# The first mixer's projections and attention: the context's query projection moved in among x's attention units

## The reference, cut to what matters

```python
aq, bq, ak, av, bk, bv = split_cols(h @ w_in, AB_SPLITS)
aq = apply_rope2d(rms_norm(aq..., a_q_norm), *rope);  ak likewise
y_a = windowed_sink_attention(aq, ak, av, ak_c, av_c, a_sink)
bq = diff_qk(bq, b_q_norm, rope);  bk likewise            # norm per head, rotation
s = einsum(q, k) * HEAD_DIM ** -0.5; p = softmax(s)       # diff_attend
w = p[:, :, 0] - lam * p[:, :, 1];   y_b = w @ v
y_b = rms_norm(y_b, b_sub_norm) * (1 - lam_init)
y = concatenate([y_a, y_b]) @ w_out
# the context: the same without rotation, over its own keys alone
```

## Time and profile before

| what | us |
|---|---|
| median of 3 runs | 2525.12 |
| profiled execution, device time | 2524.71 |
| its span | 2522.8 |
| PE busy in the span | 2451.0 (97%) |
| DVE busy | 1649.8 (65%) |
| ACT busy | 1031.2 (41%) |

### The profile page before, as it was taken

One profiled execution on the slowest core, in us unless ns is written; L12 is line 12 of the kernel. 1 busy time (PEld: TensorE's weight loads), 2 busy tenths in 40 slices (PEclk: granted clock), 3 DMA queues, 4 the chain that ended last, 5 costly groups with the idle time before them and its releaser, 6 DMA issues. The chain is left out here.

```text
span 2522.8 us, 37350 instructions
## 1 busy us (share of the span) xinstructions
PE 2451.0 (97%) x15262; PEld 2147.1 (85%) x15262; DVE 1649.8 (65%) x2728; ACT 1031.2 (41%) x1677; POOL 0.2 (0%) x4
## 2 busy tenths in 40 slices
PE   8999899999999999998899999999999999999999
PEld 8998799899978888886678888888888887879999
DVE  7667544788776677568768666548555447846553
ACT  6545544444432222356634222224222226744442
POOL 0000000000000000000000000000000000000000
PEclk9999999999999999999999999999999999999999
DMA  6545433577455555353015555425555426502554
GB/s 211 168 151 157 152 118 118 179 242 235 154 166 167 165 168 168 105 182 109 1 43 163 167 163 171 131 91 175 164 174 168 129 91 176 186 8 76 183 183 144
DMA packets 139820, 372.24 MB, mean 148 GB/s; under 512 B 22634, under 2 KB 32514, under 8 KB 139650
## 3 DMA queue, kind: packets, MB, share of 16 engines
q1 hardware_dynamic: 139362, 369.54, 47.2%
q10 hardware_dynamic: 288, 0.31, 0.0%
HBM read 368.64 MB, written 1.15 MB: 147 GB/s over the span
## 5 line engine op out<-in xcount | busy, mean ns | idle before, releaser
L348 PE MATMUL psum<-normed_hi,weights_hi 128*128 128x256 f32 (+2 forms) x2664 | 878.9, 330 | 17.6 <-ACT arena L479 4.2
L348 PE MATMUL psum<-normed_lo,weights_hi 128*128 128x256 f32 (+2 forms) x2664 | 865.0, 325 | 0.0
L348 PE MATMUL psum<-normed_hi,weights_lo 128*128 128x256 f32 (+2 forms) x2664 | 864.2, 324 | 0.0
L296 DVE TENSOR_TENSOR weights_lo<-weights_raw,weights_hi 128x1024 fp32r<-128x1024 f32 (+2 forms) x547 | 657.3, 1211 | 218.9 <-ACT weights_hi L290 216.6
L290 ACT CAST weights_hi<-weights_raw 128x1024 fp32r<-128x1024 f32 (+2 forms) x547 | 561.5, 1036 | 292.2 <-DMA weights_raw<-in_w_down 189.6
L348 PEld LDWEIGHTS psum<-normed_hi,weights_hi 128*128 128x128 f32 (+1 forms) x2664 | 507.4, 190 | 77.4 <-issue 19.1
L348 PEld LDWEIGHTS psum<-normed_hi,weights_lo 128*128 128x128 f32 (+1 forms) x2664 | 507.8, 191 | 40.8
L348 PEld LDWEIGHTS psum<-normed_lo,weights_hi 128*128 128x128 f32 (+1 forms) x2664 | 508.2, 191 | 38.2
L894 DVE SCALAR_TENSOR_TENSOR arena<-arena,cond 128x512 f32<-128x512 f32 x448 | 312.4, 747 | 10.4 <-DMA arena<-in_w_mod 5.0
L348 PE MATMUL psum<-hidden_hi,weights_hi 128*128 128x512 f32 (+1 forms) x594 | 219.4, 369 | 0.0
L348 PE MATMUL psum<-hidden_lo,weights_hi 128*128 128x512 f32 (+1 forms) x594 | 217.4, 366 | 0.0
(11 more groups left out here) (261 smaller groups left out, 2815.8 us busy)
## 6 DMA issues: line engine op xcount, KB each, us to landing
weights_raw<-in_w_gu SPq DMA_DIRECT2D x220, 512.0 KB, 3.6
arena<-in_w_mod SPq DMA_DIRECT2D x288, 256.0 KB, 3.2
weights_raw<-in_w_down SPq DMA_DIRECT2D x110, 512.0 KB, 3.5
weights_raw<-in_w_x SPq DMA_DIRECT2D x24, 512.0 KB, 3.5
weights_raw<-in_w_qk SPq DMA_DIRECT2D x24, 512.0 KB, 3.5
weights_raw<-in_w_z SPq DMA_DIRECT2D x16, 512.0 KB, 3.5
weights_raw<-in_w_g SPq DMA_DIRECT2D x16, 512.0 KB, 3.5
weights_raw<-in_w_ssm_branch SPq DMA_DIRECT2D x16, 512.0 KB, 3.5
```

The source lines that it names most:

```text
L296: ve.tensor_tensor(w_lo[:, c % RING, a], w_raw[:, c % RING, a], w_hi[:, c % RING, a].bitcast(F32), ALU.subtract).then_inc(lo_ready, 1)
L348: last = te.matmul(out, a, b, start=start and n == 0, stop=stop and n == 2)
```

## The change

x's query projection now stands ahead of x's sink keys. The context's query projection (8 chunks) leaves the list ahead of the attention and becomes side steps of the attention: chunks 0 to 3 at places 0 to 3, chunk 4 at 6, 5 at 7, 6 and 7 at 8. It uses banks 5 and 7, by a new class, with waits for the turns that use bank 7. The units are put in another order: difference pairs of tile 0, of tile 1, sink pairs of tile 0, of tile 1, then tiles 2 and 3 as before. Turns 7 to 9 (x's sink keys and sink queries) move behind the four transposes of step 6, ahead of chunk 4; the head norms of x's sink queries and sink keys end at places 0 to 4, those of the context's queries run at places 7 to 13, its turns at 12 to 15. The sub-norms of tiles 0 and 1 come at 11 to 14, their output turns at 16 to 19. The 14 fillers of steps 2 and 4 go. Unit 0 waits only for x's last groups and turn 6.

```diff
+        class LinearBeside(LinearT):
+            beside_banks = (5, 7)
+            def bank(self, g):
+                return self.beside_banks[g % 2]
+            def wait_bank(self, pe, g):
+                if g >= 2:
+                    pe.wait_ge(*bank_free[self.group + g - 2])
+                if g % 2 == 1:
+                    pe.wait_ge(*self.second_bank_free[g // 2])
...
                     pe.wait_ge(*u.probs)
+                    for event in u.turn_needs:
+                        pe.wait_ge(*event)
...
-        c_k, c_a, x_k, x_a, x_q, c_q = ab_main
+            (LinearT, x_t, "w_abk", WT, BK, 1024), (LinearT, x_t, "w_abq", WT, BQ, 1024),
+            (LinearT, x_t, "w_aba", TW, AK, 256), (LinearBeside, ctx_t, "w_abq", WT, BQ, 1024))]
+        c_k, c_a, x_k, x_q, x_a, c_q = ab_main
...
+        turn_items = turn_keys(ctx_t, 1) + turn_sink_keys(ctx_t, 3) + turn_keys(x_t, 5) + turn_queries(x_t, BQ, 0, 7)
+        turn_items += turn_sink_keys(x_t, 11) + turn_queries(x_t, AQ, 4, 9)
+        turn_items += turn_queries(ctx_t, BQ, 0, 13) + turn_queries(ctx_t, AQ, 4, 15)
+        turn_items[7].needs.append(last_of(c_q, 1))
+        c_q.second_bank_free = (turns.done(6), turns.done(9))
-        side = [(10 + j, h_steps[j]) for j in range(4)]
-        side += [(14, h_steps[4]), (15, h_steps[5])] + [(16, s) for s in t_steps[0:3]]
-        side += [(20, h_steps[6]), (20, h_steps[7])]
-        side += [(24, h_steps[8]), (24, h_steps[9])] + [(25, s) for s in t_steps[3:6]]
-        side += [(28, h_steps[10]), (28, h_steps[11]), (30, h_steps[12]), (30, h_steps[13])]
-        side += [(32, s) for s in t_steps[6:10]]
+        for pair, first_place in ((0, 6), (1, 10), (2, 14), (3, 22)):
+            side += [(first_place + n, step) for n, step in enumerate(h_steps[pair])]
+        side += [*zip((11, 12, 14, 18, 19, 26, 27), t_steps[0:7]), *zip((26, 27), h_steps[4])]
-                            *joined(down, norms, beside(steps_of(*ab_main), side))], (sums, 1)))
+                            *joined(down, norms, beside(steps_of(*ab_main[:-1]), side, per=2))],
...
+        units = difference_pairs(0, [last_of(x_q, 3), last_of(x_a, 0), last_of(x_a, 1), turns.done(6)]) + difference_pairs(1, [])
+        units += sink_pairs(0, [turns.done(9)], [last_of(c_q, n) for n in (2, 3)]) + sink_pairs(1, [])
+        for t in (2, 3):
+            units += difference_pairs(t, [turns.done(13)] if t == NT else []) + sink_pairs(t, [])
-        attend = Attend(units, s_ab, turned_ab, (6, 8))
+        attend = Attend(units, s_ab, turned_ab)
+        differences_end, sinks_end = (4, 8, 20, 28), (12, 16, 24, 32)
...
+        side = [*zip((0, 1, 2, 3), q_steps), *zip((0, 1), h_steps[4][2:]), *zip((1, 2, 3, 4), h_steps[5])]
+        side += [*zip((6, 6, 6), t_steps[7:10]), *zip((6, 7, 8, 8), q_steps[4:])]
+        side += [*zip((7, 8, 9, 10), h_steps[6]), *zip((10, 11, 12, 13), h_steps[7])]
+        side += [(11, (subs[0], 0)), (12, (subs[0], 1)), (13, (subs[1], 0)), (14, (subs[1], 1))]
+        side += [*zip((12, 13, 15, 15), t_steps[10:14])]
+        side += [*zip((16, 17, 18, 19), o_steps[0:4])]
-        in_order(beside(steps_of(attend), side, per=2))
+        in_order(beside(steps_of(attend), side, per=4))
```

More of the change, by code:

```diff
@@ L1661, in build, with __init__ @@
         class Pair:
-            def __init__(self, maps, bias, values, out, needs=(), minus_sink=None, lam=None, rows=None):
-                self.rows = rows
+            def __init__(self, maps, bias, values, out, needs=(), minus_sink=None, lam=None, rows=None,
+                         turn_needs=()):
+                self.rows, self.turn_needs = rows, turn_needs
                 self.maps, self.bias, self.values, self.out = maps, bias, values, out
@@ L1864, in heads_of @@
             return a[:, t, start:start + heads * HD].rearrange("p (h d) -> p h d", d=HD)
[L1866 to L1883, removed]
@@ new lines, in keys_of, with difference_pairs @@
+        def keys_of(t):
+            return (slice(S, 2 * S), range(NT, TT)) if t >= NT else (slice(0, 2 * S), range(TT))
+        both_rows = (slice(0, HD), slice(HD, P))
+        def difference_pairs(t, needs):
+            (keys, key_tiles), mine = keys_of(t), slice(t * P, (t + 1) * P)
+            return [Pair([(q2[a, h, mine], [k2[a, h, keys]]) for a in both_rows], None,
+                         [[ab[:, kt, BV + h * P:BV + (h + 1) * P] for kt in key_tiles]],
+                         ab[:, t, BQ + h * P:BQ + (h + 1) * P], lam=lam, needs=needs if h == 0 else ())
+                    for h in range(4)]
@@ new lines, in sink_pairs @@
+        def sink_pairs(t, needs, turn_needs=()):
+            (keys, key_tiles), mine = keys_of(t), slice(t * P, (t + 1) * P)
+            return [Pair([(q2[a, 4 + h, mine], [k2[a, 4, keys]]) for a in both_rows], no_mask if t >= NT else mask(t),
+                         [[ab[:, kt, AV + side * HD:AV + (side + 1) * HD] for kt in key_tiles] for side in range(2)],
+                         ab[:, t, AQ:AQ + 512].rearrange("p (s h d) -> p s h d", s=2, d=HD)[:, :, h, :],
+                         minus_sink=minus_sink[:, 2 * h:2 * h + 2], needs=needs if h == 0 else (),
+                         turn_needs=turn_needs if h == 0 else ())
+                    for h in range(4)]
@@ L2128, in build, with ab_projection @@
         x_t, ctx_t = (0, 1), (2, 3)
[L2129 to L2134, removed]
-        c_k, c_a, x_k, x_a, x_q, c_q = ab_main
+        def ab_projection(kind, tiles, name, width, start, columns):
+            return kind(W[name], KD, width, normed, tiles, ab[:, :, start:start + columns])
+        ab_main = [ab_projection(kind, *what) for kind, *what in (
+            (LinearT, ctx_t, "w_abk", WT, BK, 1024), (LinearT, ctx_t, "w_aba", TW, AK, 256),
+            (LinearT, x_t, "w_abk", WT, BK, 1024), (LinearT, x_t, "w_abq", WT, BQ, 1024),
+            (LinearT, x_t, "w_aba", TW, AK, 256), (LinearBeside, ctx_t, "w_abq", WT, BQ, 1024))]
+        c_k, c_a, x_k, x_q, x_a, c_q = ab_main
         for stage in ab_main:
@@ L2149, in build, with head_done @@
         head_items += [HeadItem(heads_of(ab, t, BQ, 8), 8, HD, last_of(c_q, t - 2), gain=row("bq")) for t in ctx_t]
         head_items += [HeadItem(heads_of(ab, t, AQ, 8), 8, HD, last_of(c_q, t), gain=row("aq")) for t in ctx_t]
-        heads = HeadNorms(head_items, head_space)
+        head_pairs = [HeadNorms(head_items[n:n + 2], head_space) for n in range(0, len(head_items), 2)]
+        def head_done(n):
+            return head_pairs[n // 2].done(n % 2)
         def turn_two(start, m, tiles, need, dest, scale=1.0):
@@ L2154, in turn_two @@
             return TurnItem([ab[:, t, start + (m + j) * P:start + (m + j + 1) * P] for j in range(2) for t in tiles],
-                            [heads.done(need)], dest, scale)
+                            [head_done(need)], dest, scale)
         side_of = {x_t: TOK, ctx_t: CTX}
[L2158 to L2162, removed]
@@ L2175, in build @@
+        c_q.second_bank_free = (turns.done(6), turns.done(9))
+        h_steps, t_steps = [steps_of(pair) for pair in head_pairs], steps_of(turns)
+        side = []
+        for pair, first_place in ((0, 6), (1, 10), (2, 14), (3, 22)):
+            side += [(first_place + n, step) for n, step in enumerate(h_steps[pair])]
+        side += [*zip((11, 12, 14, 18, 19, 26, 27), t_steps[0:7]), *zip((26, 27), h_steps[4])]
+        side.sort(key=lambda placed: placed[0])
         tables = GainTables(("aq", "ak", "bq", "bk"), *rope64, HD, [tables64[g] for g in ("aq", "ak", "bq", "bk")])
@@ L2186, in build @@
-        out_items = []
[L2187 to L2194, removed]
@@ L2195, in build @@
-        out_turns = Turns(out_items)
[L2196 to L2199, removed]
+                            *joined(down, norms, beside(steps_of(*ab_main[:-1]), side, per=2))],
+                           (sums, 1)))
+        units = difference_pairs(0, [last_of(x_q, 3), last_of(x_a, 0), last_of(x_a, 1), turns.done(6)]) + difference_pairs(1, [])
@@ new lines, in build @@
+        units += sink_pairs(0, [turns.done(9)], [last_of(c_q, n) for n in (2, 3)]) + sink_pairs(1, [])
[3 more added lines that the diff above has]
+        differences_end, sinks_end = (4, 8, 20, 28), (12, 16, 24, 32)
+        subs = [SubNorm(t, (aa_out, attend.base + differences_end[t])) for t in range(TT)]
+        out_items = []
+        for t, m in ((0, 4), (1, 4), (0, 0), (1, 0), (2, 4), (2, 0), (3, 4), (3, 0)):
+            at0 = AQ if m == 0 else BQ
+            need = (aa_out, attend.base + sinks_end[t]) if m == 0 else (sub_done, t + 1)
+            out_items.append(TurnItem([ab[:, t, at0 + j * P:at0 + (j + 1) * P] for j in range(4)], [need],
+                                      [n[:, m:m + 4, t * P:(t + 1) * P] for n in normed],
+                                      1.0 if m == 0 else col("b_sub"), pair=True,
+                                      busy=(5 if t == TT - 1 and m == 0 else 0, SPARE_BANK)))
```

20 lines of the change are left out of this document (9 added, 11 removed).

## The result

The changed kernel takes 2535.24 us (median of 8 runs, 2531.17 to 2543.89) against 2526.05 for the kernel before in as many runs. The ratio is 1.0040 with a 95% interval of 1.0029 to 1.0051, so it is slower, by 9 (medians) to 10 us (ratio). The profiled execution took 2534.82, its span is 2533.0, 10.2 over the span of before. The forecast was 2530, within 2518 to 2538.

A forecast was written before the change was run, and what follows sets the result against it. Hand-offs from PE to DVE to ACT and back bound the attention, neither engine full. Attention 28.9 us longer against a 25.3 earlier start gives 3.6; with 1.2 for the clock, 2529.5, taken as 2530, range 2518 to 2538.

The forecast's parts named there:

- rival D: Attention's first steps: the low clock is paid at each burst, 6.8 us in place of 1.2, 2535.6 us; chance 0.20.
- The front: Projections and seam ahead of the attention: unit 0's scores start at 1148.9, 25.3 us sooner.
- The three waits: PE's waits in the front: 0.4 and 0.6 us behind DVE's norms, about 1.0 at unit 0's scores.
- The new link: Attention's first steps: DVE's split waits for ACT's exponentials and split; PE waits 2.9, 3.8, 3.5 and 1.5 us.
- the term of the clock: Attention: half speed in PE's long waits without fillers costs 1.2 us, within bounds 0 and 5.1.
- the walk: Step-by-step pricing of the attention's queues: 79.1 us of PE's work plus 21.5 of waits, 100.6 against 71.7 before.
- The sinks: x's sink units: side work of 2.3 us a step against 1.3 free; PE waits 1.3, 0.8, 1.9, 0.2, 1.8.
- Rival B: x's sink units: side work is harmless as DVE catches up, 6.0 us of waits go, 2524 us; chance 0.18.
- around the last two turns: End of x's sink units: PE waits 1.5 us there.
- the last stretch: From unit 15 to the output projection, 42.2 us: order as before, change 0.
- Its sign: Trace, first 40 us of the attention: four or more granted-clock dips and an end past 1253 mean rival D.
- (C): Attention: chunks fill waits because DVE never stops for splits, 10 us sooner, 2515 us; chance 0.18.

The follow-up runs named there:

- c0: The changed kernel once more, unchanged, as the measure for the runs beside it: 2534.39 us, ratio 1.0032 to the kernel before.
- e2: Changed kernel with 8, 12 and 12 small matmuls that compute nothing ahead of the transposes of units 0, 1 and 3: 2533.46 us, ratio 1.0026 to before.
- e1: Changed kernel with the rotating norms of x's sink queries ahead of the chunk's split at places 0 and 1: 2533.21 us, ratio 1.0027 to before.
- e5: Changed kernel with x's second sub-norm at places 15 and 16 and the context's turn 12 at place 14: 2531.49 us, ratio 1.0016 to before.
- e3: Changed kernel with only the context's query projection put back ahead of the attention, new order kept: 2540.51 us, ratio 1.0056 to before.
- e8: Against e3, norms of x's sink queries and keys back beside the projection, turns 7 to 9 left in the attention: 2531.39 us, ratio 1.0021 to before.
- e4: Against e3, norms of x's sink queries and keys and turns 7 to 9 back beside the projection: 2527.17 us, ratio 1.0001 to before.
- e7: Changed kernel with the edits of e1, e2 and e5 together: 2527.61 us, ratio 0.9999 to before.

## Why the prediction was right, and where it was not

The direction and the stated range held. The forecast's own range, 2526 to 2534, did not: 2535.2 is the number of rival D (2535.6), and only the width left for the rivals takes it in. In the mixer 4.8 us over before were predicted and 9.7 were there (10.1 in c0).

- **The front.** Unit 0's scores were to come 70.8 us after the stall; they came after 72.0 (73.6 in c0, with its half-speed stretch at the stall). The three waits were to be 0.4, 0.6 and 1.0, together 2.0. They were 0.80 ahead of the first turn of x's keys, 0.59 ahead of the first turn of its difference queries and 0.89 at unit 0: 2.3. The other 0.9 us is work: the sum took 21.8 + 5.5 us off the front, 3.5 of them the seam's waits, so 23.8 of work, and PE's busy time fell from 92.6 to 69.7, by 22.9.
- **The new link.** DVE's stop of 2.5 us was 2.45, later ones 1.33, 1.33 and 0.88, and the transposes came at the predicted times to 0.1 us. PE's waits before them were 2.2, 2.2, 3.5 and 0.3 instead of 2.9, 3.8, 3.5 and 1.5. The first is shorter because a chunk takes 2.96 us there at full clock, from its first matmul to the scores behind it, where 2.73 was taken. The second and the fourth are shorter because PE ran a chunk, and later scores and values, at half speed and so used up part of the wait. That is the absorption that the term of the clock reckoned with. All eight chunks took 23.3 us in e2, at full clock, instead of 21.8, and most of the difference lay in waits: behind the last chunk PE was at 56.7 us in c0 and at 57.2 in the first profile, for 56.4 in the walk.
- **The sinks.** Second-copy waits of 1.15, 0.74, 1.85, 0.26 and 1.56 against 1.3, 0.8, 1.9, 0.2 and 1.8. Rival B is out. In c0 the last two were gone, because PE ran at half speed ahead of them.
- **The terms that were mis-sized** are the clock's 1.2 us and, in the first profile, the 1.5 us "around the last two turns". The latter measured 2.4 + 0.7 = 3.1 us. I had turn 13 wait for one copy; the copy of turn 12 stands on ACT behind unit 15's exponentials, and those wait for unit 15's maximum, for which DVE first had the second sub-norm to finish. ACT in order of time, the exponentials of unit 15 (the first and the last of them), the copy of turn 12, the copy of turn 13:

```profile
1240.75 0.72 ACT L1777 ACTIVATE arena<-arena,small 128x513 f32<-128x513 f32 x1 [1.82 <-DVE small L1822]
...
1241.47 0.71 ACT L1777 ACTIVATE arena<-arena,small 128x513 f32<-128x513 f32 x1
1242.09 0.19 ACT L1777 ACTIVATION_READ_ACCUMULATOR arena<-arena,small 128x1 f32 x1
1242.18 0.57 ACT L1660 ACTIVATE arena<-psum 128x512 f32<-128x512 f32 x1
1244.02 0.60 ACT L1660 ACTIVATE arena<-psum 128x512 f32<-128x512 f32 x1 [1.27 <-PE psum L1650]
```

  Behind it PE ran at 1.2 GHz, half of its 2.4, for 6.8 us, with 5.1 us of work in them and no long wait to absorb it:

```profile
1241.90:1248.70 6.80, 5.12 (x22) 4.10 (x23) 1.46 (x3) 2.31 (x7) 0.00 (x0) 0.50 0.00 0
```

  At full speed that work is half, so about 2.5 us went there, and 0.6 more at the earlier low clock (the scores behind the fifth chunk came at 43.9 instead of 43.3 in c0 and e2): 3.1 us, an estimate, where 1.2 stood for the whole clock. The extra wait of 1.6, 1.9 of the clock and 1.2 of the front are 4.7 of the 4.9 us that were missing. The trace of c0 divides them otherwise. There the two waits were 1.1 + 0.7 = 1.8, near the predicted 1.5, and the clock took 1.6 us at the stall, 1.3 among the sinks (from the transposes behind the 1.85 us wait to turn 12 13.9 us passed, for 12.6 in the first profile) and 1.7 in the last stretch (43.9 for 42.2): 4.6 for 1.2. So the clock's term was too small in both traces, while the turns' was too small in one. The prediction took the last stretch as that of before, 0, and in c0 it was not.
- **Rival D** priced every burst at the low clock. Its sign, four or more dips in the first 40 us, is absent (there were two, of 3.5 and 7 us); the end of the stretch past 1253 (1257.05) is there. That its number was met is luck, as the extra wait and the front made up a good part of it. e2 shows the price at zero where PE waits for DVE anyway, and e1, e2, e5 and the changed kernel show it in the context's units: mean clock 0.88, 0.94, 0.94 and 0.90, length 56.2, 52.9, 52.6 and 54.5. From the first to the third that is 3.6 us of length for some 7 us more at half speed (twice 0.12 of 56.2 less twice 0.06 of 52.6), half a microsecond for each. So half speed is paid for in the context's units and hardly in the first steps. The Trainium skill ("TensorE: Matmul & The Clock Gate", section "HAM oscillation — how this bites in real kernels") gives the cold penalty as half of the throttled time; the last stretch agrees with that (3.6 of 7), units 0 to 16 of e2 do not. The prediction's reading that by this page every burst of steps 0 to 5 would pay goes further than the section and than the trace: of the waits of 2.2, 2.2, 3.5 and 0.3 us there, the clock fell behind the first and the third.
- **What the text had wrong in its reasons.** It told the loss as the price of the chunks' splits in DVE's order. e3 shows that the eight chunks in the attention are a gain of about 6 us over the same order without them. What costs most is DVE's 9 us of norms for x's sinks and three serial turns (e3 to e8 to e4: 14 us of stretch), which PE's projection had covered before. They are not the whole account: e7 leaves them where the change put them and is as fast as before. The walk contained all of them at nearly right prices, but it was summed for the two versions only, never with one part taken out, so it could not say which part costs. (C) asked if DVE stops for splits; the stop was there, and yet e1, which removes most of it, moves the total by about 1 us.

## What to carry to other kernels

When work of a dense engine is moved into a stretch bound by another one, look first at what its old place was hiding: here the projection covered 9 us of DVE's norms, and taking cover and norms apart cost, in the order chosen, more than the filled waits brought. Price a bundle of moves one at a time, in both directions, by repeating the walk without each; a walk through the in-order queues gave the start times of the first 35 us to 0.1 us, so it can carry that. And before adding fillers for the clock, ask if the half-speed stretch lies in slack: if the waits behind it are longer than what it loses, it costs nothing.

## What the runs showed of the hardware

- Half speed that falls in waits costs nothing: 92.34 us at a mean granted clock of 0.93 and 92.34 at 0.96 (c0, e2).
- In a stretch with little slack it costs: the context's units, with the same matmuls, took 54.2 us at 0.91, 52.9 at 0.94 and 56.2 at 0.88 (c0, e2, e1). e1 was 3.8 us ahead of c0 at unit 3 and lost 2.0 in this last stretch. That the saving moved the low clock there is not shown, since it also stands at different places in two traces of one kernel.
- Two executions of one kernel had the low clock at different places, and stretches of the mixer differed by up to 3.1 us (unit 0 to unit 15's values: 105.7 and 102.6), while the mixer took 219.8 and 220.2 (first profile, c0).
- On ACT a copy queued behind exponentials that wait for a maximum of DVE let PE's next turn wait 2.4 us (first profile).
